# Weight sums on the DMA queue of GpSimd: copies issued one mask earlier, with semaphores of their own

## What is computed

```
xn = rmsnorm(x) * g_mix
u | q | k | v | gate_a | gate_b = xn @ w_in            (1024 -> 512+512+512+512+1024+1024)
A = pooled(u), trailing windows 2/4/8/16, mean minus token, per-group 128x128 map, scale
B: z = q.k / 8 per head (8 heads x 64), strictly causal
   a[t,s] = sigmoid(z[t,s]) * prod_{s<j<t} (1 - sigmoid(z[t,j]));  B = a @ v
x += (sigmoid(gate_a) * (A @ w_pool_up) + sigmoid(gate_b) * (B @ w_sb_up)) @ w_out
x += relu(rmsnorm(x) @ w_up)^2 @ w_down                (1024 -> 4096 -> 1024)
x += sigmoid(rmsnorm(x) @ w_ple_gate) * (p @ w_ple_proj)
y = rmsnorm(x) * g_final
```

## Time and profile before

| | us |
|---|---|
| Time, median of 3 runs | 774.92 (773.32 to 775.55) |
| Profiled execution, its own time | 772.34 |
| its span, first to last instruction | 770.6 |
| PE busy | 754.8 (98%) |
| DVE busy | 556.9 (72%) |
| ACT busy | 422.0 (55%) |
| POOL busy | 147.2 (19%) |

### The profile page before, as it was taken

One profiled execution on the slowest core, in us unless ns is written; L12 is line 12 of the kernel. 1 busy time (PEld: TensorE's weight loads), 2 busy tenths in 40 slices (PEclk: granted clock), 3 DMA queues, 4 the chain that ended last, 5 costly groups with the idle time before them and its releaser, 6 DMA issues.

```text
span 770.6 us, 14459 instructions
## 1 busy us (share of the span) xinstructions
PE 754.8 (98%) x5902; PEld 746.2 (97%) x5902; DVE 556.9 (72%) x705; ACT 422.0 (55%) x524; POOL 147.2 (19%) x259
## 2 busy tenths in 40 slices
PE   9999999999999999999999999999999999999994
PEld 9999999999999999999999999999999999999993
DVE  6776556566567527588998669965998667677986
ACT  7545535435485442477674347634763356556575
POOL 1051342453471332021110111111101000000001
PEclk9999999999999999999999999999999999999998
DMA  7254848769779899988797989789776957342503
GB/s 242 93 181 140 233 147 224 225 193 262 218 179 265 259 242 275 292 267 262 213 299 270 236 329 251 282 232 354 207 243 201 278 185 217 105 117 66 204 1 116
DMA packets 49516, 165.78 MB, mean 215 GB/s; under 512 B 6320, under 2 KB 8368, under 8 KB 49456
## 3 DMA queue, kind: packets, MB, share of 16 engines
q1 hardware_dynamic: 28512, 94.16, 35.6%
q0 software_dynamic: 18688, 67.18, 35.5%
q10 hardware_dynamic: 2256, 3.60, 1.4%
HBM read 160.39 MB, written 71.63 MB: 301 GB/s over the span
## 4 chain that ended last, share of the span: by engine, by line
PE 90%; DVE 5%; ACT 3%; issue 1%; DMA 1%; SPq 0%; POOL 0%; POOLq 0%; DVEq 0%
PE psum L1646 23%; PE psum L1697 16%; PE psum L1345 14%; PE psum L1351 14%; PE psum L1348 14%; PE psum L1394 1%; PE psum L1422 1%; DMA xt<-x_t 1%; PE psum L1420 1%; PE psum L1382 1%; PE psum L1381 1%; ACT xt L1265 1%; PE psum L1401 1%; PE psum L1406 1%; ACT L879 0%
## 5 line engine op out<-in xcount | busy, mean ns | idle before, releaser
L853 ACT ACTIVATE w_hi<-raw_more 128x1024 fp32r<-128x1024 f32 x83 | 87.7, 1056 | 72.3 <-PE psum L1697 43.3
L1345 PE MATMUL psum<-a_hi,w_hi 128*128 128x272 f32 x576 | 120.6, 291 | 0.6 <-DVE w_lo L1812 0.5
L1820 DVE TENSOR_TENSOR w_lo<-raw_more,w_hi 128x1024 fp32r<-128x1024 f32 x83 | 101.1, 1222 | 26.1 <-ACT w_hi L853 25.7
L1351 PE MATMUL psum<-a_hi,w_lo 128*128 128x272 f32 x576 | 119.3, 289 | 0.0
L1348 PE MATMUL psum<-a_lo,w_hi 128*128 128x272 f32 x576 | 118.9, 288 | 0.0
L1646 PE MATMUL psum<-u_hi,w_hi 128*128 128x272 f32 x560 | 116.4, 289 | 1.0 <-ACT h_of L1097 1.0
L1646 PE MATMUL psum<-u_hi,w_lo 128*128 128x272 f32 x560 | 115.8, 289 | 0.0
L1646 PE MATMUL psum<-u_lo,w_hi 128*128 128x272 f32 x560 | 115.7, 288 | 0.0
L1345 PEld LDWEIGHTS psum<-a_hi,w_hi 128*128 128x128 f32 x576 | 90.3, 189 | 1.1 <-DVE w_lo L1812 0.7
L1348 PEld LDWEIGHTS psum<-a_lo,w_hi 128*128 128x128 f32 x576 | 90.5, 189 | 0.0
L1351 PEld LDWEIGHTS psum<-a_hi,w_lo 128*128 128x128 f32 x576 | 90.0, 189 | 0.0
(11 more groups left out here) (287 smaller groups left out, 1553.0 us busy)
## 6 DMA issues: line engine op xcount, KB each, us to landing
sums_t<-w_tiles POOLq DMA_DIRECT2D x96, 512.0 KB, 8.2
raw<-w_tiles SPq DMA_DIRECT2D x63, 512.0 KB, 4.4
raw_more<-sums_t SPq DMA_DIRECT2D x42, 512.0 KB, 5.8
raw_more<-w_tiles SPq DMA_DIRECT2D x41, 512.0 KB, 4.5
sums_t<-sums_t POOLq DMA_DIRECT2D x32, 512.0 KB, 11.1
raw<-sums_t SPq DMA_DIRECT2D x22, 512.0 KB, 6.0
xt<-x_t SPq DMA_DIRECT2D x8, 272.0 KB, 5.7
y_t<-xt SPq DMA_DIRECT2D x16, 136.0 KB, 1.9
```

The lines of the kernel that those rows point to most:

```text
L853: act.activation(w_hi[:, t % W_RING, :, :].rearrange("p k c -> p (k c)"), src, ACT.Copy)\
L1345: pe.matmul(base[:, h, :], w_hi[:, s, wk, :], at(hi, k, h * HALF, (h + 1) * HALF), start=(opens and q == 0), stop=False, skip_group_check= ...
L1351: mm = pe.matmul(base[:, h, :], w_lo[:, s, wk, :], at(hi, k, h * HALF, (h + 1) * HALF), start=False, stop=(closes and q == len(ks) - 1), s ...
L1820: dve.tensor_tensor(w_lo[:, t % W_RING, :, :].rearrange("p k c -> p (k c)"), src, w_hi[:, t % W_RING, :, :].rearrange("p k c -> p (k c)"), ...
```

## The change

The four copies of slot k are issued between the sticks' masks (with the window sums and, in the seventh head, the window mean) and the wait for the probabilities, with nothing to wait for. The additions stay behind the probabilities' masks. The copies get two semaphores of their own, used in turn; the additions of slot k wait for the copies of slot k - 1 and for the additions of slot k - 1. `sums_in` counts additions alone. Behind the heads `sum_copies(k)` and `sum_additions(k)` are called as before, between the same waits for PE's results.

```diff
+        sums_begun = [sem("sums_begun0"), sem("sums_begun1")]
...
-            return [(i, k - i) for i in range(max(0, k - len(SUM_STEPS) + 1), min(k + 1, len(SUM_GROUPS)))]
+            return [(i, k - i) for i in range(max(0, k - len(SUM_STEPS) + 1), min(k, len(SUM_GROUPS)))]
...
             def sum_copies(k):
 
-                if 0 < k:
+                if k < len(SUM_GROUPS):
+                    for what, of in SUM_STEPS[0]:
+                        pool.dma_start(sum_tile(k, what), sum_tile(k, of)).then_inc(sums_begun[k % 2], 16)
+
+            def sum_additions(k):
+
+                if 0 < k <= len(SUM_GROUPS):
+                    pool.wait_ge(sums_begun[(k - 1) % 2], 16 * len(SUM_STEPS[0]) * ((k - 1) // 2 + 1))
+                if 1 < k:
                     pool.wait_ge(sums_in, sums_made(k - 1))
                 for i, step in sum_slot(k):
-                    if step == 0:
-                        for what, of in SUM_STEPS[0]:
-                            pool.dma_start(sum_tile(i, what), sum_tile(i, of)).then_inc(sums_in, 16)
-
-            def sum_additions(k):
-
-                for i, step in sum_slot(k):
-                    if step:
-                        for what, of in SUM_STEPS[step]:
-                            pool.dma_start(sum_tile(i, what), sum_tile(i, of), accum_op=ALU.add).then_inc(sums_in, 16)
+                    for what, of in SUM_STEPS[step]:
+                        pool.dma_start(sum_tile(i, what), sum_tile(i, of), accum_op=ALU.add).then_inc(sums_in, 16)
...
+                sum_copies(g)
                 pool.wait_ge(prob_done, g + 1)
                 mask_diagonals(pm_done)
-                sum_copies(g)
                 sum_additions(g)
```

## The result

The changed kernel took 781.7 us (median of 4 runs, 780.41 to 783.14), the kernel before 775.0 (773.32 to 775.55). The ratio is 1.0091, 95% interval 1.0066 to 1.0115: slower by 7 us, where 2.9 were forecast and 781.0 was the upper end. The profiled execution took 780.41 us, 8.07 more than that of before, with a span of 778.7.

What follows compares the result with a forecast made beforehand. PE was taken to set the time, busy 754.8 of 770.6 us. Adding 2.8 us (first head) and 0.1 (third) to 772.34 gave 775.2, or 777.8 on the median; forecast's own range 776.5 to 780, whole range 774.0 to 781.0.

Steps and rivals of the forecast that it cites:

- The path: First head: the copies delay one weight tile's load, then ACT, DVE's `prob_lo` and PE's `outputs`; PE waits 2.8 us.
- what a load pays for the copies in front of it: First head, load issued at 48.8: 3.2 us more, between 0 and 5.3, landing at 55.4 instead of 52.2.
- Rival A: First head: queues share evenly, load lands at 53.6, PE waits 1.0 us, 775.9 on the median; chance 0.22.
- The third head: Load issued at 102.5 lands late, at 111.2; PE waits 0.1 us, range 0 to 0.5.
- The seventh head: POOL has least idle time here, 0.4 us left before the probabilities' masks; masks up to 1 us later cost nothing.
- POOL's issue: Issuing four copies takes 2.08 us, now ahead of the probabilities' masks; POOL's idle time there covers it, no cost.
- the added waits: Additions of slot k wait for copies issued a whole head before, already waited for until now; no cost.
- Behind the heads: Copies of slots 9 and 10 move up about 20 us; `w_lo` has 5.8 us of room; nothing, at most 3 us.
- Rival B: Behind the heads: tile of 323.1 lands over 5.8 us later; with 3 us, 780.8 on the median; chance 0.07.
- C: Rival, faster: sums' DMAs end earlier, leaving engines to SP; PE regains at most 2.1 us, 772.8 at best; chance 0.08.
- D: Rival: the change does nothing, no load is in the way of the moved copies; 774.9 us; chance 0.13.

Runs made afterwards that it cites:

- the filled kernels: Changed kernel plus 22 extra matmuls in PE's first-head wait, 778.55 us; changed kernel with SP's next load held and 16 extra matmuls there, 778.33 us.
- the loads written out: Changed kernel with SP's loads of tiles 2 to 11 written out one by one instead of looped, none held: 780.57 us, ratio 1.0081.
- the kernel with slot 0 alone: Kernel before, with only slot 0's copies moved ahead of the first head's probabilities: 781.83 us, ratio 1.009.

## Why the prediction was wrong

**The path was right.** PE sets the time; the one place without room was `outputs` of the first head; the copies moved to 44.9; the load of the tile between `prob` and `prob_hi` was late; ACT, DVE and PE handed its delay on one to one, less the 0.43 us by which `prob_lo` was quicker. Slot 0's copies alone make the whole loss (1.009), and without them 1.0026 is left.

**The term that was mis-sized: what a load pays for the copies in front of it.** I had two rows, 5.3 us more for the load issued at 54.7 and 3.4 more for the one at 124.0, scaled both by the work left in front, and took 3.2. Six profiles measured 4.0 to 5.8 us more. The scaling was wrong. In these profiles the load did not pay a fixed share of what was left: with four copies in front it got nothing until 52, while POOL moved all (rows 10 showed just that), and then took its own time; with two, which were nearly through by then, it paid 0.6 us. Three in front were not run. Of my rows the one with four fresh copies was the like case, and its 5.3 us lie within the measured 4.0 to 5.8. I saw rows 10, used them against even sharing, and then did not use them for the size. Rival A, even sharing with a stall of 1.0 us, is refuted by the 5.25 us. By the rule of the Trainium skill, "DMA: Bandwidth & Descriptors", section "Queues, rings and completion order", the load would have shared from the start, and the trace does not agree: up to 52 SP's queue moved nothing and POOL's 0.68 MB in two us.

**The term that was left out: the clock.** I priced PE's wait at its own length. Behind 5.25 us of idleness came matmuls at 1.2 GHz that took 1.7 us more (1.5 to 1.7 in four profiles, nothing in the two with the wait filled). The medians of the filled kernels are lower by more, 3 and 6 us; what beyond the 1.7 they gain is not shown. In the trace of before PE is never idle for that long between its warm-up and its tail, so no row there priced it; it should have been a bound of its own in the range. With 5.8 - 0.4 = 5.4 for the wait and 1.7 for the clock the sum is 7.1. The measured median is 6.7 higher, but that this comes so close is in part luck: the sum is of one execution, and between the two profiled executions 8.07 us lie, 6.73 up to the end of the heads, 0.8 in the first MLP group and the rest in the tail.

**The third head.** 0.1 us was forecast, none measured in the changed kernel: its load took 7.4 us instead of 8.7. With the loads written out PE waited 0.38 us there, so the range of 0 to 0.5 held.

**The seventh head, POOL's issue and the added waits.** Nothing was forecast and nothing measured; POOL had 0.34 us left of the 0.4.

**Behind the heads.** The tile did land later (ACT waited 7.26 us instead of 4.46), short of the 5.8 us of room that I gave `w_lo`, yet PE waited 0.66 us. The copies that moved there are not what made it: alone they cost nothing (0.9991), and the kernel with slot 0 alone had 2.0 us there. What the profiles do show is that it goes with the late first head. PE's wait on `issue` at that line was 0.7, 2.0, 1.4, 0.7, 1.4 and 1.4 us in the six with four copies in front of the load, filled or not, and 0.4 us at most in the other eight, six of them with none. I took nothing for it, and how a delay at 60 us makes a wait at 365 was not found. Rival B, with its 3 us, did not happen as told. C did not either: the waits that it would have taken away are still there. D is refuted.

## What to carry to other kernels

When DMAs are moved, look for loads that will be issued just behind them, and for each ask what is in front of it in the engines and how long its consumer can wait; a load with no room at its consumer goes in front of the bulk, or the bulk is cut so that little of it is in flight (two copies here instead of four). Free time of the issuing engine says nothing about it. For a wait of some us put on a PE that was never idle, count the wait and then the time at the lower clock behind it (here 1.5 to 1.7 us for waits of 3.7 to 5.2; no wait of about 0.5 us was followed by such a loss).

## What was not expected of the hardware

Copies on POOL's queue did not share the DMA engines evenly with a load of SP: with four of 0.5 MB issued 3.6 us before it the load took 7.4 to 9.2 us, with two 4.0, with one 3.4, and with four issued 0.4 us behind it 3.6, as the first bytes of those came only two us behind their issue. And 22 matmuls without use in a wait of 5 us kept the clock at 1.00 and went with a median that was 3 us lower.
